# Recurrent branch of a two-block network: chunk products and triangular inverse of both directions issued together over four 64x64 tiles of TensorE

## What is computed

```python
def step(S, inp):
    r_t, w_t, k_t, v_t, a_t, b_t = inp
    sa = jnp.einsum('bhij,bhj->bhi', S, a_t)
    S = S * w_t[:, :, None, :] + sa[..., None] * b_t[:, :, None, :] + v_t[..., None] * k_t[:, :, None, :]
    y = jnp.einsum('bhij,bhj->bhi', S, r_t) if emit else None
    return S, y
...
S_f, y_f = rwkv_scan(states0[0], r, decay[0], k_dir[0], v, -kk, b_dir[0], False, emit)
S_b, y_b = rwkv_scan(states0[1], r, decay[1], k_dir[1], v, -kk, b_dir[1], True, emit)
```

## Time and profile before

| | |
|---|---|
| median of 3 runs | 2738.19 us (2735.17 to 2742.86) |
| the profiled execution, first to last instruction | 2737.4 us |
| PE busy | 2609.8 us (95%) |
| DVE, ACT, POOL busy | 62%, 34%, 30% |
| core stage of the first pair: chunk products | 226.1 to 241.1 us |
| its inverse | 241.1 to 270.8 us |
| its scan | 270.8 to 297.6 us |

### The profile page before, as it was taken

One profiled execution on the slowest core, in us unless ns is written; L12 is line 12 of the kernel. 1 busy time (PEld: TensorE's weight loads), 2 busy tenths in 40 slices (PEclk: granted clock), 3 DMA queues, 4 the chain that ended last, 5 costly groups with the idle time before them and its releaser, 6 DMA issues. The chain is left out here.

```text
span 2737.4 us, 60348 instructions
## 1 busy us (share of the span) xinstructions
PE 2609.8 (95%) x25068; PEld 2076.6 (76%) x25068; DVE 1708.1 (62%) x3073; ACT 929.3 (34%) x2145; POOL 834.5 (30%) x1067
## 2 busy tenths in 40 slices
PE   7999999999999999999999999999999899999998
PEld 5978798795654887868688867777888677858886
DVE  5657767764525846764653358659833676577675
ACT  2012323223422225642221148321211576122571
POOL 3323344240013520012322215235531344246010
PEclk9999999999999999999999999999999999999999
DMA  6231100102422013303111152131111311122200
GB/s 246 95 119 32 45 19 3 50 4 96 155 108 89 34 62 140 125 1 107 34 62 62 62 188 71 53 115 54 40 62 62 139 63 62 62 84 86 85 3 31
DMA packets 108432, 206.04 MB, mean 75 GB/s; under 512 B 21923, under 2 KB 26162, under 8 KB 107648
## 3 DMA queue, kind: packets, MB, share of 16 engines
q1 hardware_dynamic: 107888, 201.30, 21.0%
q0 software_dynamic: 272, 0.89, 0.1%
HBM read 186.85 MB, written 15.54 MB: 74 GB/s over the span
## 5 line engine op out<-in xcount | busy, mean ns | idle before, releaser
L739 PE MATMUL psum<-weights,h_t 128*128 128x256 f32 x1488 | 354.1, 381 | 5.5 <-ACT early_work L828 5.5
L739 PEld LDWEIGHTS psum<-weights,h_t 128*128 128x128 f32 x1488 | 280.1, 191 | 45.4 <-ACT early_work L828 6.7
L739 PE MATMUL psum<-z_l,x_tiles 128*128 128x256 f32 x816 | 192.8, 379 | 0.5 <-POOL z_l L954 0.5
L1528 DVE TENSOR_REDUCE neg_max<-psum 128x1 f32<-128x768 f32 x160 | 147.2, 955 | 67.5 <-PE psum L1304 57.2
L739 PEld LDWEIGHTS psum<-z_l,x_tiles 128*128 128x128 f32 x816 | 155.0, 190 | 21.9 <-issue 0.9
L839 ACT ACTIVATE early_work<-psum 128x512 f32<-128x512 f32 (+1 forms) x80 | 45.1, 566 | 363.8 <-DVE psum L1112 247.3
L1477 ACT ACTIVATE prob<-psum,neg_max 128x768 f32<-128x768 f32 x128 | 114.2, 897 | 79.1 <-DVE neg_max L1528 79.1
L1112 DVE TENSOR_TENSOR psum<-psum,early_work 128x512 f32<-128x512 f32 x62 | 43.2, 696 | 146.3 <-PE psum L739 146.3
L1600 POOL TENSOR_TENSOR z_l<-z_l,inv_total 128x128 f32<-128x128 f32 x64 | 25.4, 401 | 308.7 <-DVE inv_total L1536 308.7
L739 PE MATMUL psum<-weights,x_tiles 128*128 128x256 f32 x496 | 117.2, 379 | 0.0
L790 PE MATMUL psum<-weights,h_t 128*128 128x512 f32 x256 | 111.5, 593 | 1.2 <-PEq L240 1.2
(11 more groups left out here) (545 smaller groups left out, 6673.5 us busy)
## 6 DMA issues: line engine op xcount, KB each, us to landing
weights<-in_ada_w_dram SPq DMA_DIRECT2D x30, 2048.0 KB, 8.2
weights<-in_a_w_in_dram SPq DMA_DIRECT2D x10, 2048.0 KB, 7.9
weights<-in_b_w_in_dram SPq DMA_DIRECT2D x8, 2048.0 KB, 8.8
weights<-in_c_w_in_dram SPq DMA_DIRECT2D x8, 2048.0 KB, 8.6
weights<-in_w_in_dram SPq DMA_DIRECT2D x6, 2048.0 KB, 8.9
x_aside<-x_tiles SPq DMA_DIRECT2D x24, 512.0 KB, 2.6
x_tiles<-x_aside SPq DMA_DIRECT2D x4, 3072.0 KB, 15.5
weights<-in_a_w_out_dram SPq DMA_DIRECT2D x4, 2048.0 KB, 7.8
```

The source lines that it names most:

```text
L739: last = pe.matmul(dst, lhs[:, k, :], rhs[k // 2][:, k % 2, :], start=k == 0, stop=k == KH - 1)
L1528: dve.tensor_reduce(neg_max[:, i % 4, m:m + 1], score_at(i, m), AX, ALU.max, negate=True)\
```

## The change

1. **Home of the second direction.** For `d` = 1, `nt`, `bt` and `kt` write head 0 to partitions 64 to 127 and head 1 to 0 to 63 (`crosses`, `home`). Their matmuls use the two quarters off the diagonal. PE issues both directions of a chunk in turn, so these jobs and the X products go over all four quarters. P stays with its head's half, direction after direction, on two quarters at a time; `ak`, `rb`, `rk` do not cross either.
2. **Batches.** A step of the inverse takes both directions of 4 chunks: three batches a level (`batches`), 15 steps of 16 + 16 matmuls instead of 20 steps of 8 + 8 or 16 + 16 matmuls. The number of matmuls stays.
3. **Copies back.** Because X comes out uncrossed and is needed crossed, ACT copies direction 0 in one instruction and direction 1 in two of 64 partitions; the same for `bt`, `kt`.
4. **Order.** `nt`, `bt` and `rb` stand before the inverse (`ahead` = 5 jobs); `kt`, `ak` and `rk` go between its steps, one job after each of the steps 0 to 6.
5. **Start of the inverse.** One scalar_tensor_tensor with a new mask `pair` takes the place of two tensor_tensors (`begin`).
6. In the scan, W and U of direction 1 use the off-diagonal quarters.

```diff
+            def home(d, h):
+                return halves[h if d == 0 else 1 - h]
...
-    batches = [(d, seg) for d in range(2) for seg in range(2)]
-    steps = [(li, m, bi) for li, m in enumerate(LEVELS[1:]) for bi in range(4)]
+    batches = [(XC, NC), (0, XC // 2), (XC // 2, XC)]
+    steps = [(li, m, bi) for li, m in enumerate(LEVELS[1:]) for bi in range(3)]
...
+    jobs = [("nt", late, (0, 1), 0), ("nt", early, (0, 1), 2), ("bt", late, (0, 1), 4), ("bt", early, (0, 1), 6),
+            ("rb", early, (0, 1), 0)]
+    ahead = len(jobs)
+    jobs += [("kt", late, (0, 1), 0), ("kt", early, (0, 1), 0), ("ak", late, (0, 1), 0), ("ak", early, (0,), 0),
+             ("ak", early, (1,), 1), ("rk", early, (0,), 0), ("rk", early, (1,), 1)]
...
+                for c in range(a, e):
+                    for h in range(2):
+                        for d in range(2):
+                            last = pe.matmul(x_ps(i, d)[halves[h], c - a, :], n_m[li % 2][home(d, h), d, c, :],
+                                             b["inv"][home(d, h), d, c, :], start=True, stop=True)
+                last.then_inc(*x_done.tick())
...
+            for i in range(len(steps)):
+                first_product(i)
+                if i:
+                    second_product(i - 1)
+                if ahead + i < len(jobs):
+                    multiply(ahead + i)
+            second_product(len(steps) - 1)
...
-                act.activation(x_s[:, d, a:e, :], step_ps(X + i % 2, e - a, CH), ACT.Copy).then_inc(*x_out.tick())
+                act.activation(x_s[:, 0, a:e, :], x_ps(i, 0), ACT.Copy)
+                for h, s in enumerate(halves):
+                    last = act.activation(x_s[home(1, h), 1, a:e, :], x_ps(i, 1)[s], ACT.Copy)
+                last.then_inc(*x_out.tick())
+                if ahead + i < len(jobs) and jobs[ahead + i][0] == "kt":
+                    take(ahead + i)
...
+            for i in range(2):
+                for d in range(2):
+                    take(i, d)
+                for d in range(2):
+                    begin(i, d)
+                for d in range(2):
+                    mirror_begun(i, d)
+            for d in range(2):
+                take(4, d)
```

More of the change, by code:

```diff
@@ L3733, in rwkv_core_stage @@
-    v_jobs = [i for i, j in enumerate(jobs) if j[5] is not None]
-    a_jobs = [i for i, j in enumerate(jobs) if j[5] is None]
-    eye = masks[:, MASKS.index("eye"), :]
[L3737 to L3743, removed]
+    early, late = (0, XC), (XC, NC)
+    products = dict(nt=(b["b_f"], b["a_f"], "", b["m_ab_t"]), ak=(b["k_f"], b["a_f"], "", b["m_ak"]),
+                    rb=(b["b_f"], b["r_f"], "_i", b["m_rb"]), rk=(b["k_f"], b["r_f"], "_i", b["m_rk"]),
+                    bt=(b["b_f"], None, None, b["b_tok"]), kt=(b["k_f"], None, None, b["k_tok"]))
@@ L3782, in rwkv_core_stage, with multiply @@
         W, S, Y, U = 0, 2, 4, 6
-        X, B = 6, 4
         @block.tensor
         def _(pe):
[L3787 to L3791, removed]
-                    cols = slice(col_of(c), col_of(c) + CH)
[L3793 to L3797, removed]
+            def multiply(i):
+                name, (a, e), ds, _ = jobs[i]
+                left, right, _, _ = products[name]
+                for x, d in before(i):
+                    pe.wait_ge(*done(x, d))
+                for c in range(a, e):
+                    cols = slice(col_of(c), col_of(c) + CH)
+                    for h, s in enumerate(halves):
+                        for d in ds:
+                            rhs = pr.eye[s, s] if right is None else right[s, d, cols]
+                            to = home(d, h) if crosses(i, d) else s
+                            last = pe.matmul(job_ps(i, d)[to, c - a, :], left[s, d, cols], rhs, start=True, stop=True)
@@ new lines, in take, with begin @@
+                dve.tensor_tensor(out(i, d), job_ps(i, d), wide(mask, 1, e - a), ALU.mult).then_inc(*taken_v.tick())
+            def begin(i, d):
+                a, e = jobs[i][1]
+                cols = dict(two=2)
+                src = out(i, d).rearrange("p c (s two) -> p c s two", **cols)[:, :, :, 1 - d]
+                t = b["inv_t"][:, d, a:e, :].rearrange("p c (s two) -> p c s two", **cols)[:, :, :, 1 - d]
+                dve.wait_ge(*done(i, d))
+                dve.scalar_tensor_tensor(t, src, odd_row[d], wide(pair, 1, e - a), ALU.add, ALU.mult).then_inc(*begun.tick())
@@ L3954, in _ @@
+            for d in range(2):
+                take(4, d)
             for i, (li, m, bi) in enumerate(steps):
[L3955 to L3958 removed]
+                if ahead + i < len(jobs) and jobs[ahead + i][0] != "kt":
+                    for d in jobs[ahead + i][2]:
+                        take(ahead + i, d)
+                a, e = batches[bi]
```

226 lines of the change are left out of this document (112 added, 114 removed).

## The result

| | before | after |
|---|---|---|
| median | 2740.32 us (2731.17 to 2752.77, 20 runs) | 2750.90 us (2747.20 to 2758.33, 20 runs) |
| ratio to before | | 1.0042, 95% interval 1.0034 to 1.0051 |
| profiled execution, first to last instruction | 2737.4 us | 2747.0 us |
| mean granted clock | 0.994 | 0.982 |

What follows compares the result with a forecast made beforehand. PE was taken to bound products and inverse. Savings of 22.5 us there and 1.5 in the scan, 24 us off the 2737.4 us span, gave 2713.4; the median, 0.8 above the span, was forecast at 2714 us, range 2703 to 2740.

Steps and rivals of the forecast that it cites:

- rival A: Products and inverse: four tiles bring nothing, as tiles on one row strip load weights in turn; 2742 us; chance 0.18.
- C: Crossing products: tiles writing the same 64 PSUM partitions take turns, 43.8 ns a record, 2787 us; chance 0.04.
- The hole at the start: Before the inverse's first step PE idles about 3.5 us, released by DVE's takes of rb.
- DVE's chain: Ahead of the first step: DVE's takes, begins and transposes end at 8.6 us, with 0.8 for turns POOL wins.
- 768 x 14.6 = 11.2 us: Each core stage: nt, bt, kt and X, 768 records, run over four tiles at 14.6 ns each.
- 5.6: Products and inverse: gain in us taken for each stage, between 4.6 and 6.5; times four, 22.5 us.
- Rival B: PE's issue or instruction fetch sets a floor of 20 to 25 ns a record; 2722 to 2733 us; chance 0.10.
- The steps of 1.5 us: Late inverse, steps 7 to 14: PE, DVE and ACT about level, each step about 1.5 us.
- 0.1 us a chunk is all that PE holds back: Scan: crossed W and U gain at most 1.2 us a stage; 0.4 taken, 1.5 us in all.
- slower: Whole kernel: a time above the no-change band of 2730 to 2746 us; chance 0.08.

Runs made afterwards that it cites:

- Experiment 4: Changed kernel with 384 identity matmuls that wait for nothing ahead of each core stage, on four or two tiles with 32 to 128 columns; 2842.94 us.
- 3: Changed kernel with direction 0 issued before direction 1 in every crossing job and X, so only two tiles run at a time; 2750.57 us.
- 6: Changed kernel with P computed for only two of four chunks, 120 matmuls a stage fewer, inverse incomplete; 2729.56 us.
- experiment 8: Changed kernel's order and batches, but nothing crosses: all of direction 1 on its head's diagonal tile, X back in one copy a direction; 2743.23 us.
- 1: Changed kernel with W and U of direction 1 in the scan back on the diagonal tiles; 2741.31 us.
- experiment 7: Changed kernel with unread filler matmuls in PE's holes and in the scan, and W and U of direction 1 on the diagonal tiles; 2772.76 us.
- 9: Changed kernel with unread filler matmuls only ahead of the scan, and W and U of direction 1 on the diagonal tiles; 2748.46 us.
- Experiment 2: Kernel before with only W and U of direction 1 in the scan moved to the off-diagonal tiles; 2742.53 us.
- experiment 5: Changed kernel with unread filler matmuls in the hole at the start, in each step from 8 on and in the scan's context chunks; 2783.52 us.

## Why the prediction was wrong

**Right.** PE bounded products and inverse before, with its supply of instructions close behind. Four tiles pack whole: 14.5 ns a record, with the loads beside matmuls of the same rows. The rule of the Trainium skill, TensorE: Matmul & The Clock Gate, Part 3 (What overlaps and what doesn't), that was cited under rival A, does not hold here, and rival A's mechanism is out, as is C's (no record of X came slower than P's). The hole at the start had DVE's take of rb as its releaser, as forecast. That it was 2.9 us for 3.5 is in part luck: DVE's chain ended 9.6 us after the first product and not 8.6, since the begins beside POOL took 1.45 and 2.53 us, and PE came to the hole 1.8 us late, mostly by its own pause of 1.46. The number of records is unchanged.

**The step that failed: "768 x 14.6 = 11.2 us".** The 14.6 ns hold for 128 records between two pauses, and for the first 183 of a stage; over a stage the supply gives one in 28. 1472 records at 28 ns are 41.2 us; the hole and the last step alone come on top, and 43.0 to 45.4 were measured. Experiment 4 measures this price by itself, 3 shows that the array's gain is worth at most some 0.6 us a stage in place of 5.6, and 6 that fewer instructions do shorten the stage. Rival B named the fetch of instructions with a floor of 20 to 25 ns and a chance of 0.10; the mechanism was right, but the price too low: 27 to 29 ns were measured, block for block. The bound that the trace did hold was left unused: no stretch of before goes under 29 ns for long. Such a row says that *something* ends there, and the array was only the first candidate. The steps of 1.5 us in the second half of the inverse became 1.8 to 2.0 (3.58 to 4.05 us for two). That the clock of products and inverse, too, was lower for a while (0.88 and 0.89 in stage 1) cost the rest: stage 2, at 1.00 throughout, is 1.75 us shorter than stage 1, though executions of one code differ by as much.

**The term that was missing: the clock.** It stood at 1.00 in every row read, and the sum treated it as given. Yet the scan was read as "0.1 us a chunk is all that PE holds back", a gain of 1.5 us, when the crossing takes busy time from PE in a chain that it doesn't shorten. Where the clock stays up, the crossed scan is indeed faster: one chunk of both directions in the sequence's part takes 2.03 to 2.04 us in after, 2.09 in before. But 10 to 14 us of each scan run at the lower level, and the price is 9.0 us in the scans. The 3.1 in a prepare stage are not shown to come of the change: experiment 8, which crosses nothing, has such a fall behind another scan. But one regularity stands in the traces: in all seven executions in which the clock fell in or ahead of the first scan (after, 1 to 6) it fell again in the prepare stage behind it, and in none of the four others (before, 7, 8, 9). Experiment 2 shows the crossing as a cause that suffices, 1 and 9 the idle time ahead of the scan as another; without both (8, 9) all eight scans take 26.4 us.

**The sum,** by what was measured: -2.2 for products and inverse (within the scatter), +9.0 in the scans, +3.1 in the prepare stage, -0.3 at the start. The forecast's range, 2703 to 2740, missed the time; slower had been given 0.08, and only for mechanisms that did not occur.

**Open:** why the clock in experiment 7's stage 2 and experiment 5's stage 3 stayed down for 27 and 41 us; what sets 3.45 us in one place and 3.73 in another between two arrivals of instructions (the packets themselves took 0.94 to 1.18); and what brings the clock down in the prepare stages, where executions differ. No version was found that beats the kernel before: two tiles (29.2 ns) and the supply of instructions (27 to 29 ns a record) end close to each other, so only fewer instructions would help, and 6 is no kernel that computes the inverse.

## What to carry to other kernels

Before paying for more tiles, divide the bytes of the instruction queue by its records, and time the packets: a stream of small fp32 matmuls on two tiles already takes them as fast as they come, and then only fewer and larger instructions help, not a freer array. A tight stream is no proof of which limit ends it; a stream of a few hundred matmuls that wait for nothing tells in one run. And work that is packed side by side in a chain which it can't shorten lowers PE's busy time, which here took the clock from up to half of the chain: count a lower granted clock as a term wherever a change thins PE out, ahead of the chain too.

## What the runs showed that was not expected

- PE's instructions come in packets of 16.4 KB, 64 fp32 matmuls, every 3.45 to 3.75 us in a stream that waits for nothing; 128 records on four tiles run in 1.95 us, and PE then pauses for 1.1 to 1.8.
- Moving 32 columns or 64 on four tiles takes about the same time in a long stream (20.0 us, more than half of it at the lower clock, and 19.3 for 768 records), 128 columns only a fifth more (23.2).
- One code, two executions: products and inverse of the four stages took 178.9 and 176.7 us in the kernel before, 176.6 and 181.2 in the changed one. A gain of 2 us there shows in no single pair of profiles.
- The same 63 or 64 records spread over four tiles instead of two, with 2.25 us busy in place of 2.67, and the clock went to its lower level for 10.2 us.
- A matmul of the full array between 64x64 tiles cost a chain 0.32 to 0.34 us each.
